# Every buffer that TensorE reads in the large products begins at a multiple of 2048 bytes

## The chip, the cores and the metric

The kernel runs on one core of one Trainium2 chip. The metric is device time in microseconds, the median of several runs. On the core, TensorE multiplies, VectorE and ScalarE work on the results and prepare operands, GpSimd does small work and issues some transfers, and SyncE issues the loads of the weights. All of them share an on-chip memory of 128 partitions; an address in this text is a byte offset inside a partition, the same in all 128.

## The reference

One inference step of a two-layer backbone over two streams of 128 tokens (context and latent) of width 1024. Each layer has a mixer (four kinds of attention behind one input projection of 2400 columns and one output projection) and a channel mixer: dense SwiGLU of width 2816 in layer 0, eight experts of width 3584 with two chosen per token in layer 1. Everything is float32.

```python
sh1, sc1, gt1, sh2, sc2, gt2 = _modulation(silu_cond, w_ada[l], b_ada[l])
h = _rmsnorm(x, norm_mix_pre[l]) * (1.0 + sc1) + sh1
x = x + gt1 * _rmsnorm(mixer(h) @ w_o[l], norm_mix_post[l])
h = _rmsnorm(x, norm_ffn_pre[l]) * (1.0 + sc2) + sh2
# layer 0: (silu(h @ wg) * (h @ wu)) @ wd ; layer 1: the same for 8 experts, summed with their gates
x = x + gt2 * _rmsnorm(channel_mixer(h), norm_ffn_post[l])
```

## The kernel before

**Units.** The weights come from HBM in units of [128, 2048] floats, 1 MB, into six raw buffers (`raw`, line 536 issues the loads on SyncE). A product of full precision is made of three fast ones: ScalarE rounds the unit to a high part (`w_hi`, line 841, `hi`), VectorE takes the difference as a low part (`w_lo`, line 1239, `lo`), and TensorE adds up high x high, low x high and high x low. The activations are split in the same way into `x_hi`, `x_lo` (1024 columns for each of two streams) and `h_hi`, `h_lo` (512 columns, the hidden layer).

**The products.** `products` (lines 1791 to 1800, experts and dense feed-forward) and `products_of` (lines 1802 to 1818, the projections and the last units of the dense stage) run over the tiles of a unit. Lines 1794/1809 multiply `x_hi` by `w_hi`, 1795/1810 `x_lo` by `w_hi`, and then, once the low part is there, 1799/1816 `x_hi` by `w_lo`. In each matmul the activation is the stationary operand, 128 x 128 (512 bytes per partition), and the weights are streamed through: 512 columns (2048 bytes) in the experts, the down units and the output projections, 256 in the dense gate and up units, 480 in the input projection. A unit of the experts is 4 tiles, so 8 high products and then 4 low ones.

**Slots.** A split unit lies in one of three slots; `slot(c)` (line 174) says which: slots 0 and 1 are in `w_hi` and `w_lo`, slot 2 is `w_hi3`, `w_lo3`, laid over `qz` (which attention uses), and slot 3, used once, lies in `region`. In the experts the slot is `-c % 3`. A block of the expert loop has the units up, up, down, down, gate, gate in TensorE's order after the transposes of line 2240, in slots 2, 1, 0, 2, 1, 0. In the dense stage gate units (before the transposes of line 2108) lie in slot 0, up units (after them) in slot 1, down units in slot 2, except the last down unit, which lies in slot 0.

**Where the buffers begin.** Buffers are laid one after the other, each rounded up to 32 bytes. The change puts 1920 bytes (`mod` 768, `small` 1024, `fill` 128) ahead of `raw` and asserts that the next address is a multiple of 2048, so memory begins 128 bytes past one. From the order of the declarations follow the distances past the last multiple of 2048:

| buffer | before | after |
|---|---|---|
| `raw`, `w_hi`, `w_lo` (slots 0, 1) | 128 | 0 |
| `region` (also slot 3 and `y_hi`, `y_lo`) | 128 | 0 |
| `w_hi3`, `w_lo3` over `qz` (slot 2) | 768 | 0 |
| `x_hi`, `x_lo` | 448 | 0 |
| `h_hi`, `h_lo` | 768 | 0 |
| `x`, `xn`, `cond`, `mrow` | 448 | 0 |
| `cst` (identity for the transposes) | 640 | 512 |

## Time and profile before

| | |
|---|---|
| median of 3 runs | 1540.9 us (1540.82 to 1544.19) |
| span of the profiled execution | 1541.9 us |
| TensorE matmuls | 1490.1 us busy, 97% |
| VectorE | 1155.6 us, 75% |
| ScalarE | 974.6 us, 63% |
| HBM | 317 GB/s over the span |

The stages in order of time are: the modulation and input projection of layer 0 (to about 75 us), attention and output projection (to 190), the dense feed-forward (190 to 376), layer 1 up to its router (376 to 558), the eight experts (558 to 1539). Matmuls are pipelined: a recorded matmul of 512 columns lasts about 390 ns, but the next one begins some 230 ns after it began. So the busy time of TensorE says that it is never idle, and not whether its matmuls follow each other as closely as they can. The chain that ended last is the view for that: it counts each piece from its beginning to the beginning of what follows.

### The profile page before, as it was taken

How to read it: one execution, taken by the hardware profiler on the slowest of the kernel's cores; microseconds unless marked ns; L12 is line 12 of the kernel's file. 1: busy time of each engine (PE TensorE's matmuls, PEld its weight loads, DVE VectorE, ACT ScalarE, POOL GpSimd, SP SyncE). 2: the span in 40 equal slices, each digit the busy share in tenths (PEclk: the TensorE clock that was granted, in tenths of full speed). 3: DMA queues.
4: the chain of work that ended last, by engine and by line, in shares of the span. 5: the costliest groups of instructions: out<-in, count | busy, mean ns of one | idle time of the engine just before them, and what ended most of it. 6: DMA issues, size and time to landing. Idle time of an engine off the chain costs nothing.

```text
span 1541.9 us, 21865 instructions
## 1 busy us (share of the span) xinstructions
PE 1490.1 (97%) x7705; PEld 1216.6 (79%) x7705; DVE 1155.6 (75%) x990; ACT 974.6 (63%) x959; POOL 125.2 (8%) x180
## 2 busy tenths in 40 slices
PE   6999999999998999999999999999999999999995
PEld 3867799996876788888878878878878887887884
DVE  2577554445667478888888888888888888888885
ACT  3555533445455457777777777777777777777773
POOL 2421410000021200000000000000000000000001
PEclk9999999999999899999999999999999999999998
DMA  8976986558661879999999999999999999999991
GB/s 327 343 267 200 333 264 198 174 189 290 241 211 60 323 279 366 396 365 392 367 346 394 375 355 382 374 356 373 381 369 360 385 369 357 386 371 342 395 386 50
DMA packets 222629, 489.13 MB, mean 317 GB/s; under 512 B 9040, under 2 KB 42144, under 8 KB 222576
## 3 DMA queue, kind: packets, MB, share of 16 engines
q1 hardware_dynamic: 215024, 466.38, 83.6%
q0 software_dynamic: 7552, 22.03, 4.7%
q8 instruction: 34, 0.56, 0.1%
q14 instruction: 19, 0.16, 0.0%
HBM read 479.53 MB, written 8.85 MB: 317 GB/s over the span
## 4 chain that ended last, share of the span: by engine, by line
PE 93%; DVE 3%; ACT 2%; issue 1%; DMA 1%; POOL 0%; POOLq 0%; SPq 0%; DVEq 0%; ACTq 0%
PE ps L1794 24%; PE ps L1799 24%; PE ps L1795 24%; PE ps L1809 4%; PE ps L1816 3%; PE ps L1810 3%; PE ps L1840 2%; PE ps L2240 2%; PE ps L2019 1%; DMA raw<-in_w_ada 1%; PE ps L1972 1%; PE ps L1851 1%; PE ps L1994 1%; PE ps L1896 1%; PE ps L1863 1%
## 5 line engine op out<-in xcount | busy, mean ns | idle before, releaser
L1239 DVE TENSOR_TENSOR w_lo<-raw,w_hi 128x2048 fp32r<-128x2048 f32 (+1 forms) x397 | 905.4, 2285 | 192.1 <-ACT w_hi L841 191.8
L841 ACT ACTIVATE w_hi<-raw 128x2048 fp32r<-128x2048 f32 (+1 forms) x397 | 757.8, 1914 | 255.7 <-PE ps L1795 236.2
L1794 PE MATMUL ps<-w_hi,x_hi 128*128 128x512 f32 (+1 forms) x1216 | 434.7, 369 | 1.4 <-DVE region L1465 1.4
L1795 PE MATMUL ps<-w_hi,x_lo 128*128 128x512 f32 (+1 forms) x1216 | 426.9, 363 | 0.0
L1799 PE MATMUL ps<-w_lo,x_hi 128*128 128x512 f32 (+1 forms) x1216 | 284.6, 364 | 0.0
L1794 PEld LDWEIGHTS ps<-w_hi,x_hi 128*128 128x128 f32 x1216 | 228.8, 188 | 40.6 <-DVE region L1465 1.6
L1795 PEld LDWEIGHTS ps<-w_hi,x_lo 128*128 128x128 f32 x1216 | 228.8, 188 | 36.4
L1799 PEld LDWEIGHTS ps<-w_lo,x_hi 128*128 128x128 f32 x1216 | 206.9, 188 | 39.6
L1794 PE MATMUL ps<-w_hi,h_hi 128*128 128x512 f32 x520 | 204.6, 393 | 4.9 <-DVE h_lo L1579 4.3
L1795 PE MATMUL ps<-w_hi,h_lo 128*128 128x512 f32 x520 | 204.3, 393 | 0.0
L1799 PE MATMUL ps<-w_lo,h_hi 128*128 128x512 f32 x520 | 139.0, 392 | 0.0
L1794 PEld LDWEIGHTS ps<-w_hi,h_hi 128*128 128x128 f32 x520 | 97.7, 188 | 28.2 <-issue 5.7
L1799 PEld LDWEIGHTS ps<-w_lo,h_hi 128*128 128x128 f32 x520 | 97.9, 188 | 21.5
L1795 PEld LDWEIGHTS ps<-w_hi,h_lo 128*128 128x128 f32 x520 | 97.8, 188 | 21.5
L1809 PE MATMUL ps<-w_hi,x_hi 128*128 128x480 f32 (+2 forms) x256 | 96.4, 382 | 5.0 <-ACT x_hi L906 4.5
L1810 PE MATMUL ps<-w_hi,x_lo 128*128 128x480 f32 (+2 forms) x256 | 94.6, 375 | 0.0
L1816 PE MATMUL ps<-w_lo,x_hi 128*128 128x480 f32 (+2 forms) x256 | 63.9, 374 | 0.0
L1809 PEld LDWEIGHTS ps<-w_hi,x_hi 128*128 128x128 f32 x256 | 49.1, 192 | 18.2 <-ACT x_hi L906 6.1
L809 POOL DMA_INDIRECT region<-h_rows,from_row x7 | 8.4, 1196 | 635.4 <-PE ps L2205 635.1
L1810 PEld LDWEIGHTS ps<-w_hi,x_lo 128*128 128x128 f32 x256 | 49.0, 191 | 7.0
L1840 PE MATMUL ps<-raw,cond 128*32 128x512 f32 x384 | 51.7, 639 | 2.8 <-DMA raw<-in_w_ada 1.9
L982 ACT ACTIVATE h_hi<-ps 128x512 fp32r<-128x512 f32 x11 | 6.6, 601 | 74.8 <-PE ps L2108 74.8
(271 smaller groups left out, 1086.6 us busy)
## 6 DMA issues: line engine op xcount, KB each, us to landing
raw<-in_moe_w_gate SPq DMA_DIRECT2D x112, 1024.0 KB, 7.3
raw<-in_moe_w_up SPq DMA_DIRECT2D x112, 1024.0 KB, 7.3
raw<-in_moe_w_down SPq DMA_DIRECT2D x112, 1024.0 KB, 7.2
raw<-in_w_ada SPq DMA_DIRECT2D x48, 1024.0 KB, 7.5
raw<-in_w_in SPq DMA_DIRECT2D x20, 960.0 KB, 7.7
raw<-in_ffn_w_gate SPq DMA_DIRECT2D x11, 1024.0 KB, 5.4
raw<-in_ffn_w_up SPq DMA_DIRECT2D x11, 1024.0 KB, 6.4
raw<-in_ffn_w_down SPq DMA_DIRECT2D x11, 1024.0 KB, 5.3
```

What stands on the lines that cost most here:

```text
L841: act.activation(split_hi(c, slice(0, width(c))), raw[:, r % NRAW, 0:width(c)], ACT.Copy).then_inc(hi_done, 1)
L1239: dve.tensor_sub(split_lo(c, n), raw[:, raw_of(c) % NRAW, n], split_hi(c, n)).then_inc(lo_done, 1)
L1794: pe.matmul(out, xh, split_hi(c, w), start=start, stop=False, skip_group_check=True)
L1795: last = pe.matmul(out, xl, split_hi(c, w), start=False, stop=False, skip_group_check=True)
L1799: last = pe.matmul(out, xh, split_lo(c, w), start=False, stop=stop, skip_group_check=True)
L1809: pe.matmul(out, xh, split_hi(c, w), start=start, stop=False, skip_group_check=True)
L1810: last = pe.matmul(out, xl, split_hi(c, w), start=False, stop=False, skip_group_check=True)
L1816: last = pe.matmul(out, xh, split_lo(c, w), start=False, stop=stop, skip_group_check=True)
L1840: last = pe.matmul(row_ps(m)[CG * kt:CG * kt + CG, :], cond[:, 4 * h + kt, i, :], raw[:, r % NRAW, 512 * kt:512 * kt + 512], start=first, ...
L1851: last = pe.matmul(col_ps(l, k)[:, 4 * kt:4 * kt + 4], mrow[:, m % 2, P * kt:P * kt + P], cst[:, C_SEL:C_SEL + 4], start=True, stop=True)
L1863: last = pe.transpose(ps[:, T_bank(l, which, s) + k // 4, cols(k % 4, P)], xn[:, s, cols(k, P)], ident())
L2240: last = pe.transpose(ps[:, 0, cols(r, P)], hid[:, cols(r, P)], ident())
```

## The change

The list of allocations is reordered and nothing else is edited: `mod`, `small` and an unused buffer `fill` of 128 bytes stand first, so that `raw` begins at a multiple of 2048; then come `raw`, `w_hi`, `w_lo`, `qz` (with `w_hi3`, `w_lo3`), `x_hi` (with `probs`), `x_lo`, `h_hi`, `h_lo`, `x`, `xn`, `cond`, `mrow`, whose sizes are all multiples of 2048, then `region`, and the small buffers behind it. Instructions, their order, shapes, waits and transfers stay as they are; only addresses differ.

```diff
+BLOCK_B = 2048
...
+        mod = sb("mod", [P, DEPTH, 6, KT, 2])
+        small = sb("small", [P, 256])
+        sb("fill", [P, 32])
+        assert nc.sbuf_base % BLOCK_B == 0, nc.sbuf_base
         raw = sb("raw", [P, NRAW, UNIT])
         w_hi = sb("w_hi", [P, NSPL - 1, UNIT], F32R)
         w_lo = sb("w_lo", [P, NSPL - 1, UNIT], F32R)
+        qz_at = nc.sbuf_base
+        qz = sb("qz", [P, 6, 2, 4, P])
+        w_hi3 = nc.alloc_sbuf_tensor_at("w_hi3", [P, UNIT], F32R, offset=qz_at)
+        w_lo3 = nc.alloc_sbuf_tensor_at("w_lo3", [P, UNIT], F32R, offset=qz_at + 4 * UNIT)
+        x_hi_at = nc.sbuf_base
+        x_hi = sb("x_hi", [P, 2, D], F32R)
+        probs_all = nc.alloc_sbuf_tensor_at("probs", [P, 2, 2, 4, 256], F32, offset=x_hi_at)
+        x_lo = sb("x_lo", [P, 2, D], F32R)
+        h_hi = sb("h_hi", [P, 512], F32R)
+        h_lo = sb("h_lo", [P, 512], F32R)
+        x = sb("x", [P, 2, D])
+        xn = sb("xn", [P, 2, D])
+        cond = sb("cond", [P, KT, 2, CG])
+        mrow = sb("mrow", [P, 2, 512])
+        assert nc.sbuf_base % BLOCK_B == 0, nc.sbuf_base
         REGION = 11904
         region_at = nc.sbuf_base
         region = sb("region", [P, REGION])
...
         cst = sb("cst", [P, C_N])
-        x = sb("x", [P, 2, D])
-        xn = sb("xn", [P, 2, D])
-        x_hi_at = nc.sbuf_base
-        x_hi = sb("x_hi", [P, 2, D], F32R)
...
-        x_lo = sb("x_lo", [P, 2, D], F32R)
-        cond = sb("cond", [P, KT, 2, CG])
-        mrow = sb("mrow", [P, 2, 512])
-        mod = sb("mod", [P, DEPTH, 6, KT, 2])
...
-        small = sb("small", [P, 256])
...
-        qz_at = nc.sbuf_base
-        qz = sb("qz", [P, 6, 2, 4, P])
...
-        h_hi = sb("h_hi", [P, 512], F32R)
-        h_lo = sb("h_lo", [P, 512], F32R)
```

## Rows read from the trace of the kernel before

**Rows 1.** The page: busy time, the chain by engine and line, loads

```profile
PE 1490.1 (97%) x7705; PEld 1216.6 (79%) x7705; DVE 1155.6 (75%) x990; ACT 974.6 (63%) x959; POOL 125.2 (8%) x180
...
PE 93%; DVE 3%; ACT 2%; issue 1%; DMA 1%; POOL 0%; POOLq 0%; SPq 0%; DVEq 0%; ACTq 0%
PE ps L1794 24%; PE ps L1799 24%; PE ps L1795 24%; PE ps L1809 4%; PE ps L1816 3%; PE ps L1810 3%; PE ps L1840 2%; PE ps L2240 2%; PE ps L2019 1%; DMA raw<-in_w_ada 1%; PE ps L1972 1%; PE ps L1851 1%; PE ps L1994 1%; PE ps L1896 1%; PE ps L1863 1%
...
raw<-in_moe_w_down SPq DMA_DIRECT2D x112, 1024.0 KB, 7.2
raw<-in_w_ada SPq DMA_DIRECT2D x48, 1024.0 KB, 7.5
```

**Rows 2.** Busy time by stage, with granted clock, DMA share and GB/s

```profile
core 0: us, PE busy (x) PEld busy (x) DVE busy (x) ACT busy (x) POOL busy (x), PEclk, DMA share, GB/s
...
190.00:376.00 186.00, 182.94 (x1325) 169.86 (x1327) 90.20 (x61) 72.19 (x58) 9.45 (x18) 1.00 0.66 217
...
520.00:541.00 21.00, 19.48 (x119) 15.19 (x117) 9.57 (x27) 13.81 (x24) 4.77 (x10) 0.71 0.88 325
541.00:558.00 17.00, 15.78 (x78) 13.83 (x78) 12.42 (x20) 10.06 (x8) 0.00 (x0) 0.86 0.60 211
558.00:1539.00 981.00, 962.55 (x4311) 783.08 (x4309) 844.30 (x486) 704.68 (x470) 30.50 (x23) 0.99 0.98 359
600.00:640.00 40.00, 40.00 (x181) 32.57 (x180) 34.70 (x19) 29.54 (x21) 0.00 (x0) 1.00 1.04 393
```

**Rows 3.** Waits, 700 to 1400 us, load queue apart: total, times, longest

```profile
ACT w_hi L841 <- PE ps L1795: 174.1, 230, 0.9
DVE w_lo L1239 <- ACT w_hi L841: 90.4, 197, 1.0
...
PE ps L1794 <- DVE h_lo L1579: 4.3, 6, 0.7
...
SPq L536 <- DVE w_lo L1239: 537.3, 241, 4.9
```

**Rows 4.** Chain in order of time, one expert block: start us, us

```profile
602.71 0.44 PE ps L2240 x4
...
604.99 0.92 PE ps L1799 x4
...
607.76 0.93 PE ps L1799 x4
...
610.55 0.94 PE ps L1799 x4
...
613.32 0.91 PE ps L1799 x4
...
616.09 0.93 PE ps L1799 x4
...
618.89 0.94 PE ps L1799 x4
619.83 0.44 PE ps L2240 x4
```

**Rows 5.** Chain, dense stage: up, down, gate, up, gate, the last down

```profile
204.30 1.81 PE ps L1799 x16
...
209.74 1.81 PE ps L1799 x8
...
215.32 1.89 PE ps L1799 x16
...
221.64 1.89 PE ps L1799 x16
...
232.76 1.89 PE ps L1799 x16
...
372.08 0.93 PE ps L1816 x4
```

**Rows 6.** Chain: input projection (480 columns), output projection (512 columns)

```profile
81.84 0.87 PE ps L1816 x4
...
163.44 0.93 PE ps L1816 x4
```

**Rows 7.** Chain: the first load

```profile
2.33 15.26 DMA raw<-in_w_ada
```

**Rows 8.** Timeline of ScalarE and VectorE in the experts: start us, us

```profile
737.66 1.92 ACT L841 ACTIVATE w_hi<-raw 128x2048 fp32r<-128x2048 f32 x1 [0.86 <-PE ps L1795]
...
736.93 2.29 DVE L1239 TENSOR_TENSOR w_lo<-raw,w_hi 128x2048 fp32r<-128x2048 f32 x1 [0.47 <-ACT w_hi L841]
...
744.63 0.68 DVE L1579 TENSOR_TENSOR h_lo<-ps,h_hi 128x512 fp32r<-128x512 f32 x1
```

More of the change, by code:

```diff
@@ L270, in program @@
         cst = sb("cst", [P, C_N])
-        x = sb("x", [P, 2, D])
-        xn = sb("xn", [P, 2, D])
-        x_hi_at = nc.sbuf_base
-        x_hi = sb("x_hi", [P, 2, D], F32R)
-        probs_all = nc.alloc_sbuf_tensor_at("probs", [P, 2, 2, 4, 256], F32, offset=x_hi_at)
-        x_lo = sb("x_lo", [P, 2, D], F32R)
-        cond = sb("cond", [P, KT, 2, CG])
-        mrow = sb("mrow", [P, 2, 512])
-        mod = sb("mod", [P, DEPTH, 6, KT, 2])
         mtmp = sb("mtmp", [P, KT, 2])
@@ L288, in program @@
         lam = sb("lam", [P, 8])
-        qz_at = nc.sbuf_base
-        qz = sb("qz", [P, 6, 2, 4, P])
-        w_hi3 = nc.alloc_sbuf_tensor_at("w_hi3", [P, UNIT], F32R, offset=qz_at)
-        w_lo3 = nc.alloc_sbuf_tensor_at("w_lo3", [P, UNIT], F32R, offset=qz_at + 4 * UNIT)
-        h_hi = sb("h_hi", [P, 512], F32R)
-        h_lo = sb("h_lo", [P, 512], F32R)
         pos = sb("pos", [P, 2, 2, NE + 1])
```

## The prediction

> **What bounds the kernel now.** I read the page first, then the busy time by stage, then the waits, then the chain in order of time. TensorE's matmuls are busy 1490.1 of 1541.9 us and the chain that ended last is 93% TensorE, three quarters of it the six lines that multiply by the split weights [rows 1]. By stage, the expert stage (558 to 1539) holds 981 us with matmuls busy for 962.55, the dense feed-forward stage 186 us with 182.94 [rows 2]. In the experts nobody makes TensorE wait: six waits for `h_lo`, 4.3 us in 700 us; ScalarE, VectorE and the load queue all wait for somebody who waits for TensorE [rows 3]. So the end is set by how far apart the starts of the matmuls lie, not by their recorded duration (393 ns), which overlaps the next one. I call that distance the pitch. The chain gives it, since it counts each matmul only until the next starts.
>
> **What the pitch depends on.** A block of the expert loop runs from transposes to transposes, 602.71 to 619.83: 17.12 us, of which 0.44 is the four transposes and 16.68 is 72 products, 231.7 ns each [rows 4]. The four low products at the end of each unit take 0.92, 0.93, 0.94, 0.91, 0.93, 0.94 us. That is an order of three. By the slot rule the six units (up, up, down, down, gate, gate) lie in slots 2, 1, 0, 2, 1, 0: the two short ones are the two in slot 2. Slots 0 and 1 begin 128 bytes past a multiple of 2048, slot 2 begins 768 past, which is a multiple of 256. The stationary columns begin at 448 plus multiples of 512 for `x_hi` (0.92) and at 768 plus multiples of 512 for `h_hi` (0.91). So both on multiples of 256 gives the shortest.
>
> The dense stage says it better. Its down units stand in slot 2 with `h_hi`: eight products in 1.81 us, 226.3 ns each. Only the last one stands in slot 0, with the same stationary buffer and lengths (it goes through `products_of`, four low products at a time): 0.93 for four, 232.5 [rows 5]. That pair is the ground of this forecast: move the streamed weights from 128 to a multiple of 256, in step with the stationary columns, and the pitch falls by about 6 ns. At 256 columns there are two speeds at the very same addresses: the up units at 204.30 and 221.64 take 1.81 and 1.89 us for sixteen, 113.1 or 118.1 ns [rows 5]. So an offset of 128 does not force the slow pitch; it lets the stream fall into it. Nothing in the trace begins at 0 with stationary columns at 0. The nearest row is the one at 768 with 768: equal offsets, as every product with 512 columns will have after the change.
>
> **The change, part by part.** It adds no instruction and no wait; all times come from the pitch.
> - *Experts.* 8 experts x 42 units x 12 = 4032 products. From 231.7 to 226.3 is 5.4 ns, 21.8 us in all. That is the upper end of what the rows support; the lower end is zero, and below zero in the rival. I take 85% of it, since a unit right after transposes or a wait needs a few products to fall into step: 18.5 us.
> - *Dense stage.* 11 gate and 11 up units x 48 = 1056 products of 256 columns, at 118.1 in the gate units (215.32, 232.76) and some up units, at 113.1 in the rest. If 14 of the 22 units lose 5.0 ns per product: 14 x 48 x 5.0 = 3.4 us at most; down units gain nothing. Taken: 2.2.
> - *Output projections.* Two layers x 4 units x 2 streams x 12 = 192 products at 232 [rows 6], 5.7 ns each: 1.1 us, taken 1.0; between layers the neighbours can take part of it.
> - *Input projections.* 480 products of 480 columns at 217.5 ns [rows 6]; scaled from 226.3 the good pitch is 212.2, so 2.5 us at most. But a chunk begins every 1920 bytes, so of four chunks the second and fourth will lie 128 past a multiple of 256, where before it was the first and third. Taken: 0.3, bounds -2.5 and 2.5.
> - *Loads.* `raw` moves from 128 to 0. The loads wait in the chain once, 15.26 us before the first matmul [rows 7]. The median loads of 1024 KB differ by 4% between their kinds, 7.2 and 7.5 us [rows 1], and 4 to 6% of 15.26 is under 1 us: taken 0, bounds -1 and 1. The Trainium skill ("DMA: Bandwidth & Descriptors", How a descriptor splits into AXI transactions) says that a descriptor which doesn't start on 256 bytes needs one transaction more: for rows of 2048 bytes 68 beats instead of 64, if it holds for the written side too. By that the first wait would be an estimated 0.9 us shorter. No row here compares the two.
> - *Everything else that is moved* (`cst`, `small`, `mod`, `xn`, the gaps in `region`): transposes run at 0.44 us for four, 110 ns, much longer than their 128 columns would need at this stream's rate, so the start of `cst` hardly shows. VectorE's and ScalarE's passes have the same shapes: 0. For a price if wrong: 56 blocks x 0.44 us = 25 us of transposes, 5% of it 1.2 us either way.
>
> Sum: 18.5 + 2.2 + 1.0 + 0.3 = 22.0 us. The profiled execution of before has a span of 1541.9, the median of the three runs is 1540.9, so a profile of after should have a span near 1519.9 and the median should be 1518.9.
>
> **Who is late next.** A block would last 17.12 - 72 x 0.0054 = 16.73 us. ScalarE needs 6 x 1.92, VectorE 6 x 2.29 = 13.7 plus two or three passes of 0.68, about 15.3 [rows 8]: both fit. Loads: 6.29 MB per block need 16.0 us at the 393 GB/s that the stage reaches when it has fallen behind, against 359 on the mean [rows 2]. They still fit, with 0.7 us to spare where there was 1.1. At expert boundaries the queue runs dry and the reserve is eaten; I leave 0 for it and up to 3 us as a bound. The clock: TensorE's granted clock is 0.71 and 0.86 in the stretches 520 to 541 and 541 to 558 [rows 2], a share of them at 1.2 GHz while the router runs. With all that comes before some 3 us earlier, the low stretch may shift against the products; bound 3 us either way.
>
> **Rivals.**
> - *No effect of the start.* Then the slots differ by something else that stays (the second operand's distance, the bank of the result, what the other engines write at the time) and the time stays 1540.9. The Trainium skill ("TensorE: Matmul & The Clock Gate", Part 2) has TensorE read the streamed and the stationary operand through two independent ports, so that loading the next columns takes nothing from the running matmul; and "SBUF — State Buffer" (Operand start alignment) asks only for a multiple of the element size, and says that this is about legality, not speed. By these pages the result is this rival. What speaks against it is the last down unit of the dense stage against the ten before it [rows 5]; what speaks for it is that identical addresses show both 113 and 118 ns [rows 5].
> - *Slower: everything in step is the bad case.* The mechanism is a clash between the streamed columns and the stationary columns read at the same time. If it depends on the absolute start and not on equal offsets, then buffers that all begin at 0 clash in all three slots, and slot 2 loses what it has. Price: 112 slot 2 units in the experts x 12 x (234 - 228.7) = 7.1 us; 10 down units x 24 x 6.2 = 1.5; eight quick up units x 48 x 5.0 = 1.9. Together 10.5, so 1551.4. It decides as soon as the low products of slot 2 take 0.93 or more. For it: in slots 0 and 1 the second chunk of 480 columns begins exactly at a multiple of 2048 (128 + 1920), and that stage runs at 217.5 ns where 212.2 would be the good rate. Against it: 768 with 768 is just as much in step, and it is the best case of the trace.
> - *Half of it.* Only the streamed operand counts: all units behave like slot 2 does now, 0.92 with `x_hi` in four of six and 0.91 with `h_hi` in two, 229.2 on the mean. 4032 x 2.5 = 10.1, plus half of the rest, 12 us: 1529.
> - *More than the trace has ever shown.* If 226.3 is itself held up by the streamed buffer crossing a multiple of 2048 (768 + 2048 crosses one, 0 + 2048 doesn't), the pitch could go towards 512 / 2.4 = 213 ns. Then loads would set a block at 16.0 us: 56 x 1.1 = 62 us at most, and about half of it with the boundaries: 1505 or so.
>
> **How the numbers follow.** The forecast has a chance of 0.55; half of it 0.12; no effect 0.12; slower 0.14; more 0.07. A difference of 0.3% (4.6 us) is about what a measurement of this kernel tells from none. Faster by more than that: 0.55 + 0.12 + 0.07 = 0.74; within it 0.12; slower 0.14. The forecast's own range is 1513 to 1527 (85% taken as 60% to 100%, the 3 us of the clock and the 3 us of the loads). To hold 8 in 10 the range reaches down to 1511 and up past no effect to 1542; what is left out is the slower case and most of the much faster one, 0.19.
>
> **What would show it.** In the chain of after, the low products of the six units of a block should read 0.91 each instead of 0.92, 0.93, 0.94, and transposes to transposes 16.7. The dense stage's sixteen should read 1.81 in up as in gate, and its last down unit 0.91 for four. Wrong would be: blocks of 17.12 (no effect); low products of 0.93 or 0.94 in slot 2 (slower); waits of ScalarE for `raw` in the experts (loads are the bound); a low clock in a stretch where it was full.

## The result, and the profile after

The changed kernel takes 1527.2 us (median of 4 runs, 1526.15 to 1529.33) where the kernel before took 1542.6 beside it (4 runs): a ratio of 0.990 [0.9886, 0.9911], 15.4 us less. The forecast was 1518.9, 22.0 us below the 1540.9 known then. The profiled executions have spans of 1524.5 and 1541.9, 17.4 apart.

The page of after, busy time and the chain by engine. It answers [rows 1]; every line number is 4 higher, so L1798 is what L1794 was.

```profile
PE 1471.9 (97%) x7705; PEld 1216.1 (80%) x7705; DVE 1153.6 (76%) x990; ACT 974.4 (64%) x959; POOL 124.9 (8%) x180
...
PE 92%; DVE 3%; ACT 2%; issue 1%; DMA 1%; POOL 0%; POOLq 0%; SPq 0%; DVEq 0%; ACTq 0%
```

The same instructions in the same numbers, and TensorE still sets the end. VectorE and ScalarE are as busy as before; only TensorE's 7705 matmuls are shorter, by 18.2 us.

The chain in order of time, one expert block (start us, us, what), answering [rows 4]:

```profile
601.56 0.44 PE ps L2244 x4
...
603.85 0.91 PE ps L1803 x4
...
606.57 0.91 PE ps L1803 x4
...
609.29 0.91 PE ps L1803 x4
...
612.01 0.91 PE ps L1803 x4
...
614.73 0.91 PE ps L1803 x4
...
617.45 0.91 PE ps L1803 x4
618.36 0.44 PE ps L2244 x4
```

All six units of the block now show 0.91 for their four low products, and transposes to transposes is 16.80 us instead of 17.12. The next block has a 0.92 in its first unit, which comes right after the transposes. Over the blocks of the trace the five later units run at 226.7 ns a product. The first unit, which starts slowly behind the transposes, has 237.2 on the mean where it had 236.8: it gained nothing.

The chain in the dense stage, an up unit, a down unit, a gate and an up unit, then the last down unit, answering [rows 5]:

```profile
201.94 1.92 PE ps L1803 x16
...
207.51 1.81 PE ps L1803 x8
...
213.16 1.92 PE ps L1803 x16
...
219.57 1.92 PE ps L1803 x16
...
373.35 0.92 PE ps L1820 x4
```

Here the forecast fails: sixteen products of 256 columns take 1.92 us, 120 ns each, where before some units showed 1.81 and others 1.89. The down units keep their 1.81 for eight, and the last one fell from 0.93 to 0.92.

Busy time by stage, as [rows 2] (us, busy time and count of each engine, granted clock, DMA share, GB/s): the dense stage, the experts, and 40 us of the experts:

```profile
190.00:376.00 186.00, 183.62 (x1299) 171.19 (x1300) 88.31 (x59) 71.36 (x56) 5.91 (x12) 1.00 0.62 206
...
558.00:1522.00 964.00, 944.96 (x4310) 781.60 (x4308) 842.38 (x486) 704.56 (x470) 30.05 (x23) 0.99 0.98 366
590.00:630.00 40.00, 40.00 (x181) 33.10 (x181) 35.72 (x20) 29.79 (x19) 0.00 (x0) 1.00 1.04 414
```

In the same 186 us TensorE began 1299 matmuls where it had begun 1325. The last line says that the loads, when they have fallen behind and run without a break, move 414 GB/s; before it was 393 in [rows 2] and is 394 in this stretch (its line stands at the end of the experiments).

**Where the 17.4 us went.** Times from the starts of the first and last matmul of each kind, in both traces, in us:

| stretch | before | after | difference | forecast |
|---|---|---|---|---|
| start to first product of 480 columns | 27.69 | 25.60 | -2.1 | 0 |
| input projection, layer 0 | 59.84 | 58.99 | -0.85 | -0.3 (both layers) |
| attention, output projection, layer 0 | 91.96 | 91.83 | -0.1 | -0.5 |
| dense stage, 256-column products first to last | 182.68 | 187.03 | **+4.35** | **-2.2** |
| last dense product to the end of layer 1's input projection | 75.77 | 75.51 | -0.3 | 0 |
| attention, output projection, router, layer 1 | 109.83 | 108.58 | -1.25 | -0.5 |
| experts, first to last product | 976.67 | 959.32 | **-17.35** | **-18.5** |
| end | 17.46 | 17.63 | +0.2 | 0 |

The mean pitch (start of a matmul to the start of the next, within runs of the same length) gives the same: products with `x_hi`, `x_lo` in the experts 232.0 to 227.4 ns, with `h_hi`, `h_lo` 230.7 to 226.9, output projections 232.3 to 227.9, dense products of 256 columns 115.6 to 119.8. 2688 x 4.6 + 1344 x 3.8 ns are 17.5 us in the experts, and 1056 x 4.2 ns are 4.4 us in the dense stage.

### The profile page after: what moved, and what is told of

Same layout as the page of the kernel before. It is cut to its first block, busy times and chain, and to the rows that moved or that the text cites. A ratio compares the mean times of both kernels' runs of the same rounds, so it can differ in the third digit from the quotient of the medians.

```text
span 1524.5 us, 21865 instructions
## 1 busy us (share of the span) xinstructions
PE 1471.9 (97%) x7705; PEld 1216.1 (80%) x7705; DVE 1153.6 (76%) x990; ACT 974.4 (64%) x959; POOL 124.9 (8%) x180
## 4 chain that ended last, share of the span: by engine, by line
PE 92%; DVE 3%; ACT 2%; issue 1%; DMA 1%; POOL 0%; POOLq 0%; SPq 0%; DVEq 0%; ACTq 0%
PE ps L1798 24%; PE ps L1799 24%; PE ps L1803 24%; PE ps L1813 4%; PE ps L1814 3%; PE ps L1820 3%; PE ps L1844 2%; PE ps L2244 2%; PE ps L2023 1%; DMA raw<-in_w_ada 1%; PE ps L1976 1%; PE ps L1998 1%; PE ps L1900 1%; PE ps L1855 1%; PE ps L1867 1%
## 5 line engine op out<-in xcount | busy, mean ns | idle before, releaser
L1798 PE MATMUL ps<-w_hi,x_hi 128*128 128x512 f32 (+1 forms) x1216 | 432.1, 366 | 1.4 <-DVE region L1469 1.4
L1798 PEld LDWEIGHTS ps<-w_hi,x_hi 128*128 128x128 f32 x1216 | 229.6, 189 | 36.5 <-DVE region L1469 1.6
L1798 PE MATMUL ps<-w_hi,h_hi 128*128 128x512 f32 x520 | 203.3, 391 | 4.9 <-DVE h_lo L1583 4.3
L1798 PEld LDWEIGHTS ps<-w_hi,h_hi 128*128 128x128 f32 x520 | 97.7, 188 | 26.2 <-issue 5.7
```

The costliest lines, as they stand in the source:

```text
L1798: pe.matmul(out, xh, split_hi(c, w), start=start, stop=False, skip_group_check=True)
```

## What the experiments had to tell

Three readings were left. The absolute start counts: a multiple of 256 or of 2048 bytes is what helps. Or only the difference between the starts of the stationary and of the streamed operand counts. Or neither: what the other engines read and write at the time shifts with the addresses. From here on "distance" is the start of the stationary columns minus the start of the streamed ones, modulo 256 bytes. Times stand beside runs of the kernel before on the same chip. A kernel's edit is against after unless it says otherwise.

### All at 128, and one of the two moved

All in step, but 128 bytes past a multiple of 256 (`e1_all128`; the two asserts go as well):

```diff
-        sb("fill", [P, 32])
+        sb("fill", [P, 64])
```

> The changed kernel with all its buffers moved 128 bytes further on (128 more bytes ahead of raw), so that streamed and stationary operands still begin at equal offsets, but at 128 past a multiple of 2048 instead of 0. Theory A (equal offsets count, the absolute start doesn't): the low products of an expert block read 0.91 us in all six units, the sixteen low products of the dense gate and up units 1.92, the span is that of the changed kernel, 1524.5 within 2 us. Theory B (the absolute multiple counts, as the change says): 0.93 to 0.94 as in slots 0 and 1 before, span 1540 or more.

Only the streamed weights at 128, all three slots, everything else at 0 (`e2_w128`):

```diff
         raw = sb("raw", [P, NRAW, UNIT])
+        sb("pad1", [P, 32])
         w_hi = sb("w_hi", [P, NSPL - 1, UNIT], F32R)
         w_lo = sb("w_lo", [P, NSPL - 1, UNIT], F32R)
         qz_at = nc.sbuf_base
         qz = sb("qz", [P, 6, 2, 4, P])
...
+        sb("pad2", [P, 480])
         x_hi_at = nc.sbuf_base
```

> The changed kernel with only the streamed weights (w_hi, w_lo and slot 2) moved to 128 past a multiple of 2048; x_hi, x_lo, h_hi, h_lo and everything behind stay at 0. Theory A (equal offsets): the pitch rises, low products 0.93 or more in all six units of an expert block, dense gate and up units below 1.92 because the distance is no longer 0; span 1535 to 1545. Theory B (absolute multiple of the streamed operand) says the same for the experts. If only the start of the stationary operand counted, everything would stay at 0.91 and 1524.5.

Only the stationary `x_hi`, `x_lo`, `h_hi`, `h_lo` at 448 (`e3_x448`):

```diff
+        sb("pad1", [P, 112])
         x_hi_at = nc.sbuf_base
...
         h_lo = sb("h_lo", [P, 512], F32R)
+        sb("pad2", [P, 400])
         x = sb("x", [P, 2, D])
```

> The changed kernel with only the stationary operands (x_hi, x_lo, h_hi, h_lo) moved to 448 past a multiple of 2048, where x_hi began before; the streamed weights stay at 0. Theory A (equal offsets): low products of the experts 0.92 to 0.94, dense gate and up units 1.81 to 1.89 instead of 1.92, span 1527 to 1540. If only the streamed operand's multiple counts: 0.91 in all six units of an expert block, span within 3 us of 1524.5, dense unchanged at 1.92.

| | time, us | ratio | experts, us | dense, us |
|---|---|---|---|---|
| all at 128 | 1530.4 | 0.9919 [0.989, 0.9948] | 959.39 | 187.0 |
| streamed at 128 | 1548.5 | 1.0035 [1.002, 1.0051] | 979.72 | 187.06 |
| stationary at 448 | 1531.0 | 0.9918 [0.9894, 0.9942] | 966.49 | 182.26 |

Three chains in order of time, each with low products of an expert unit and sixteen of the dense stage. All at 128:

```profile
214.49 1.92 PE ps L1801 x16
...
604.49 0.91 PE ps L1801 x4
```

Streamed at 128:

```profile
214.31 1.90 PE ps L1805 x16
...
600.58 0.94 PE ps L1805 x4
```

Stationary at 448:

```profile
213.99 1.82 PE ps L1805 x16
...
604.77 0.92 PE ps L1805 x4
```

With everything at 128 the experts and the dense stage are those of after to 0.1 us: between 0 and 128 the absolute start doesn't count. The span, 1528.2, is 3.7 us above the 1524.5 that was expected within 2; where they lie is said under the clock. Streamed at 128 the span is 1546.6, a little above the expected range. With one operand moved against the other the stages follow, and not both in the same order: distance 0 is the best of the three in the experts but no better than distance 128 (streamed at 128) in the dense stage, and distance 192 (stationary at 448) is in the middle in the experts and the best in the dense stage. The dense stage holds both lengths: its products of 256 columns run at 118.8 ns at distance 128 against 119.8 in after, and its down units, of 512 columns, take back what that gains. At distance 192 the mean is 114.9 ns, and 14 of the stage's 24 stretches of these products, gate and up alike, end at 113.3.

### The distance by itself

To take the other engines out, a kernel that only runs chains of matmuls in the order of `products`, from two buffers filled with a constant, on TensorE alone; outputs are zeros and nothing of the reference is computed. The other engines are done before the first pair of starts begins. Its loop, with `m` and `s` the starts of the streamed and the stationary columns (`p1_grid`):

```python
for k in range(n):
    wk = w[:, m + W * k:m + W * k + W]
    pe.matmul(o, xs[:, 0, s + P * k:s + P * k + P], wk, ...)
    pe.matmul(o, xs[:, 1, s2 + P * k:s2 + P * k + P], wk, ...)
for k in range(n):
    pe.matmul(o, xs[:, 0, s + P * k:s + P * k + P], w[:, 4096 + m + W * k:4096 + m + W * k + W], ...)
```

> Not the model: nothing of the reference is computed, the outputs are filled with zeros. TensorE alone repeats the kernel's pattern of products (high x high, low x high, then high x low; stationary 128 columns, streamed 512 or 256) three times for each pair of starts, streamed at 0, 64, 128, 256, 384, 768, 1024 (512 columns) or 0 to 512 (256 columns), stationary at 0 to 448 in steps of 64, four transposes between the pairs. No other engine writes meanwhile. Theory A (equal offsets): the pitch at 512 columns is the same along lines of equal distance and lowest, 226.7 ns, at distance 0; at 256 columns 120 ns at distance 0 and 113 to 118 elsewhere. Theory B (absolute multiples of 256): 226.7 only where the streamed start is a multiple of 256. Theory C (what the other engines write at the time makes the difference): 226.7 everywhere.

The chain of this kernel in order of time: low products with both starts at 0, then, after four transposes, with the stationary columns 64 bytes further:

```profile
45.20 0.91 PE ps L81 x4
46.11 0.44 PE ps L72 x4
...
48.42 0.93 PE ps L81 x4
...
54.02 0.93 PE ps L81 x4
```

Pitch in ns from the starts, 56 pairs of starts at 512 columns (streamed at 0, 64, 128, 256, 384, 768, 1024) and 48 at 256 columns, in the last of the three rounds that each pair runs (the first, right after the transposes, is slower at every distance):

| distance | 0 | 64 | 128 | 192 |
|---|---|---|---|---|
| 512 columns | 226.6 | 233.1 | 231.8 (up to 233.7 in four pairs) | 228.9 |
| 256 columns | 120.0 | 117.8 (113.3 in three of twelve pairs) | 118.8 (120.0 in one) | 117.8 |

At distances 0 and 192 rows agree to 0.3 ns whatever the start of the streamed columns is, beyond 256 bytes too; at 128, and at 64 with 256 columns, a few pairs stand apart. No other engine works while these chains run, so the others are not the cause of the differences between them.

The distance explains most of the kernel before without a free number. Slots 0 and 1 with `x_hi` lie 448 - 128 = 320 apart, distance 64: 233. Slot 2 with `x_hi`: 448 - 768, distance 192: 229. Two up and two gate units stand in slots 2, 1, 1, 0, so the mean should be (229 + 3 x 233) / 4 = 232.0; measured 232.0. Slot 2 with `h_hi`, distance 0: 226.6, the dense stage's 226.3 of [rows 5]. It does not explain the down units of the experts: slot 0 with `h_hi` is distance 128 and slot 2 distance 0, which makes 229.2 on the mean, and 230.7 was measured. The unit in slot 0 has 232.5 as it should; the one in slot 2, which follows it without a pause, has 229.0 and not 226.6, while in after, where all neighbours have distance 0 too, it has 226.7. What runs just before counts as well.

### Finer, and the order of what comes before

The same kernel with steps of 16 bytes, 480 columns, different starts for the high and the low stationary columns, and 256 columns once after transposes and once straight behind 512-column products (`p2_fine`):

```diff
+COMBOS = [(0, s, s, 256, 3, 1) for s in range(0, 256, 16)] + \
+    [c for s in range(0, 256, 16) for c in ((0, 0, 0, 512, 2, 1), (0, s, s, 256, 3, 0))] + \
+    [(0, s, s, 512, 3, 1) for s in range(0, 256, 16)] + \
+    [(0, s, s, 480, 3, 1) for s in range(0, 256, 32)] + \
+    [(0, s, s2, 256, 3, 1) for s in range(0, 256, 64) for s2 in range(0, 256, 64)]
```

> Again only TensorE's pattern of products, outputs are zeros. Streamed at 0, stationary from 0 to 240 in steps of 16, at 256 columns (once right after transposes, once right after 24 products of 512 columns without a pause), at 512 and 480 columns, and at 256 columns with the two stationary operands (high and low part) at different starts, 0, 64, 128 or 192 each. Theory A: at 512 columns a curve of the distance with its minimum of 226.7 only at 0 and a jump to 231 or more within one or two steps; at 256 columns 120 at distance 0 and at least one distance where 113.3 is reached however the sequence begins. Theory D (256 columns have two states at any distance but 0 and the start decides): the two series at 256 columns differ at the same distance.

| distance | 0 | 16 | 48 | 64 | 80 | 128 | 176 | 192 | 208 | 240 |
|---|---|---|---|---|---|---|---|---|---|---|
| 512 columns | 226.6 | 233.4 | 233.4 | 233.5 | 232.3 | 233.0 | 229.5 | 228.6 | 233.3 | 226.7 |
| 256 columns after transposes | 120.0 | 118.3 | 117.8 | **113.3** | 118.7 | 118.9 | 118.1 | 117.8 | 116.7 | 117.2 |

At 512 columns 0 and 240 are alone at the bottom, and 176 to 192 is a second, higher one. At 480 columns every distance gives 216 to 220. At 256 columns there are two speeds for the same addresses. The chain in order of time, distance 64 after transposes:

```profile
72.92 0.44 PE ps L75 x4
...
75.19 0.91 PE ps L84 x8
...
77.91 0.91 PE ps L84 x8
...
80.63 0.91 PE ps L84 x8
```

and the same distance straight behind products of 512 columns:

```profile
243.10 0.91 PE ps L84 x4
...
245.89 0.94 PE ps L84 x8
...
248.72 0.94 PE ps L84 x8
...
251.55 0.94 PE ps L84 x8
```

Eight in 0.91 are 113.3 ns each, eight in 0.94 are 117.8. Neither speed gives way to the other within 72 products. That is the 1.81 beside 1.89 at the same addresses in [rows 5]. But transposes or no transposes is not what decides: both up units of [rows 5] follow transposes, and the first of these two kernels (`p1_grid`) has the very same pair, streamed at 0 and stationary at 64, at 117.8 ns right after four transposes:

```profile
536.26 0.44 PE ps L72 x4
...
538.58 0.94 PE ps L81 x8
```

Nor is distance 64 alone in this: distance 192 has 117.8 in every row of the grid, but 113.3 in most units of the kernel with the stationary columns at 448, gate units straight behind products of 512 columns among them. What decides between the two stays open. With the high columns at distance 64 and the low ones at 192, 113.3 comes from the first products on, with 192 and 64 from the second round on, the first having 118.7; the other pairs of different starts have 116.8 to 119.1.

### What of the change is needed

Two pads in the kernel before, 384 bytes, and its order of memory otherwise (`e4_old_order`). All operands of the experts, the down units and the output projections then lie at distance 0, none at a multiple of 256:

```diff
         xn = sb("xn", [P, 2, D])
+        sb("pad1", [P, 48])
         x_hi_at = nc.sbuf_base
...
         lam = sb("lam", [P, 8])
+        sb("pad2", [P, 48])
         qz_at = nc.sbuf_base
```

> The kernel before with its old order of the memory and nothing at a multiple of 2048: 192 unused bytes ahead of x_hi and 192 ahead of qz, so that x_hi, x_lo begin at 640, slot 2, h_hi and h_lo at 1152, and slots 0 and 1 stay at 128. All the distances between streamed and stationary starts are then multiples of 256. Theory A as the grid puts it (only the distance modulo 256 bytes counts): the gain of the change comes back in full with 384 bytes of padding: low products of the experts 0.91 in all units, dense gate and up units 1.92 for sixteen, span within 4 us of 1524.5, ratio to the kernel before 0.989 to 0.992. If the order, the multiples of 2048 or 512 counted: low products of 0.92 to 0.94 in part of the units and a time above 1532.

Measured 1530.3 us, ratio 0.9905 [0.9883, 0.9926]; experts 959.40 us, dense stage 187.04, pitches 226.9 and 227.4 as in after. The span, 1529.3, is 0.8 us above what was expected, for the same reasons as with all at 128. The new order and the multiple of 2048 are not needed for what the experts gain. What after has beyond this is in the loads and the clock, below.

After once more, unedited, as the base of the next three (`e0_after`):

> The changed kernel again, unedited, as the yardstick on the same chip for the two that follow. Both theories: the same as on record, 1526 to 1530 us, dense stage 187.0 us from its first to its last product of 256 columns, experts 959.3.

1528.4 us, 0.9907 [0.9891, 0.9924].

### The dense stage given back

If distance 64 at 256 columns can reach 113.3 ns, the gate and up units have to lie 192 bytes further, and nothing else (`e5_dense64`; the slots are made 64 floats longer):

```diff
+        def at(c, n):
+            o = 48 if FFN_U + 2 <= c < MOE_U and SPLIT[c][2] < 3 * NFF - 1 and (SPLIT[c][2] + 1) % 3 < 2 else 0
+            return slice(n.start + o, n.stop + o)
...
-            return w_hi[:, slot(c), n] if slot(c) < 2 else w_hi3[:, n]
+            return w_hi[:, slot(c), at(c, n)] if slot(c) < 2 else w_hi3[:, n]
```

> The changed kernel, but gate and up units of the dense stage in slots 0 and 1 are written and read 192 bytes into their slot (slots are 256 bytes longer), so that the stationary operands begin 64 past the streamed ones modulo 256, as before the change, in this stage only; all products of 512 columns keep distance 0. Theory A (distance modulo 256, and 256 columns want another distance than 512): the dense stage goes back to 182.7 us from 187.0 (pitch 115.7 instead of 119.9, some units at 113, some at 118), experts stay at 959.3, the whole is 4.3 us quicker than the changed kernel. If the loss in the dense stage came from something else in the new order, it stays at 187.0.

Then `x_lo` of the dense stage 128 bytes further, for the pair of 64 and 192 (`e6_dense_best`):

```diff
+        def lo_at(l, which, n):
+            o = 32 if which and not l else 0
+            return slice(n.start + o, n.stop + o)
...
-            def xcols(s, k):
-                return x_hi[:, s, P * k:P * k + P], x_lo[:, s, P * k:P * k + P]
+            def xcols(s, k, dense=False):
+                o = 32 if dense else 0
+                return x_hi[:, s, P * k:P * k + P], x_lo[:, s, P * k + o:P * k + P + o]
```

> As the kernel before this one, and besides x_lo is written and read 128 bytes further on in the dense stage, so that the high stationary part begins 64 and the low one 192 past the streamed start, the pair that gave 113.3 ns from its first products on in the second grid. Theory A: the pitch at 256 columns is 113.4 in all but the first two units, the sixteen low products 1.81 us in up and gate units alike, dense stage 180.3 us, the whole 6.5 us quicker than the changed kernel. Theory D (two states at the same distance, the start decides): gate units, which follow products of 512 columns without a pause, stay at 117.8 and only up units reach 113.3; then 182 to 183 us.

In both of these the condition also caught layer 1's projection units in slots 0 and 1, which was not meant: layer 1's output projections ran at 232.3 ns instead of 227.6 to 228.0. The third has the condition mended and the two slots apart, gate units 192 bytes in (distances 64 and 192), up units 64 bytes in (192 and 64) (`e7_dense_two`):

```diff
+            o = 0
+            if FFN_U + 2 <= c < MOE_U and SPLIT[c][0] == "ffn" and SPLIT[c][2] < 3 * NFF - 1:
+                o = (48, 16, 0)[(SPLIT[c][2] + 1) % 3]
```

> As the last kernel (x_lo 128 bytes further on in the dense stage), but with a start of its own for each kind of unit: gate units 192 bytes into their slot, so that the stationary parts begin 64 and 192 past the streamed start, up units 64 bytes into it, so that they begin 192 and 64 behind it modulo 256. Projection units of layer 1, which the last two kernels had moved 192 bytes as well, are back at distance 0. Theory D (which pair of distances reaches 113.3 ns depends on how the unit begins; the grid has 192 and 64 at 113.3 right after transposes): up units reach 113.3 within their first ten products, gate units as before, dense stage 180.5 us or less, output projection of layer 1 back at 227 ns, whole 1521 to 1523 us, 6 us quicker than the changed kernel. Theory A alone says nothing about the order of the two; if the start isn't what decides, up units stay at 120 in their high products and the dense stage at 183.

| | time, us | ratio | dense, us | mean pitch, ns |
|---|---|---|---|---|
| after, edited nowhere | 1528.4 | 0.9907 [0.9891, 0.9924] | 187.03 | 119.8 |
| 64 for both | 1524.2 | 0.9877 [0.986, 0.9893] | 182.59 | 115.7 |
| 64 and 192 | 1524.0 | 0.9879 [0.9862, 0.9895] | 182.99 | 116.1 |
| two slots apart | 1523.7 | 0.9861 [0.9844, 0.9878] | 181.37 | 114.4 |

The chain of each in order of time, one gate and one up unit. Distance 64 for both:

```profile
212.18 1.89 PE ps L1807 x16
...
218.36 1.81 PE ps L1807 x16
```

64 and 192:

```profile
211.27 1.81 PE ps L1811 x16
...
217.58 1.83 PE ps L1811 x16
```

Two slots apart:

```profile
214.17 1.82 PE ps L1813 x16
...
220.28 1.81 PE ps L1813 x16
```

The first gives up units 113.3 and gate units 117.8, as expected. The second missed the 180.3 of one reading; the other had named 182 to 183, but with slow gate and quick up units, and it came the other way round: gate units have 113.7 and 113.3 in high and low products, up units 120 in their high ones. In the third the low products are at 113.3 in all but the first four stretches, which the edit leaves where they were, and one more; it ends at 181.37 and 1523.7, not quite at the 180.5 and the 1521 to 1523 expected. So 4.0 to 5.7 us come back in the dense stage, the experts stay at 959.4 in all three, and the third is faster than both given kernels: its interval ends at 0.9878 where that of after, repeated, begins at 0.9891.

### Looking for the mechanism

If the loading of the stationary columns clashes with the stream, fewer stationary columns should clash less, and the curve over the distance should keep its place. If the streamed start has a part of its own, equal starts should differ. 128, 96, 64 and 32 stationary columns, equal starts at other steps, and the streamed start alone (`p3_cols`, again without the reference's computation):

```diff
+COMBOS = [(0, s, s, 512, 3, 1, C) for C in (128, 96, 64, 32) for s in (0, 64, 128, 192)] + \
+    [(m, m, m, 512, 3, 1, 128) for m in (16, 32, 48, 80, 112)] + [(m, 0, 0, 512, 3, 1, 128) for m in (16, 32, 48, 240)] + \
+    [(m, m, m, 256, 3, 1, 128) for m in (16, 32, 48)] + [(0, s, s, 256, 3, 1, 64) for s in (0, 64, 128, 192)]
```

> TensorE's pattern alone, outputs are zeros. 512 streamed columns with 128, 96, 64 or 32 stationary columns at distances 0, 64, 128, 192; equal starts that are not multiples of 64 (16, 32, 48, 80, 112) and streamed starts of 16, 32, 48, 240 with stationary at 0; 256 columns at equal starts of 16, 32, 48, and with 64 stationary columns. Theory E (what costs is the reading of the stationary columns beside the streamed ones, a clash that the distance decides): the excess over the lowest pitch shrinks with the stationary columns, from 6 ns at 128 to about 1.5 at 32, and 256 columns at distance 0 fall from 120 towards 115 with 64. Theory F (the distance acts on the streamed read alone): the excess doesn't depend on the number of stationary columns. Equal starts off 64: 226.7 if only the distance counts, more if a multiple of 64 is needed as well.

| stationary columns, 512 streamed | distance 0 | 64 | 128 | 192 |
|---|---|---|---|---|
| 128 | 226.6 | 233.1 | 231.8 | 228.9 |
| 96 | 230.2 | 228.6 | 226.6 | 233.1 |
| 64 | 229.6 | 233.0 | 230.8 | 228.5 |
| 32 | 231.7 | 231.7 | 230.1 | 231.9 |

The spread over the four distances is 6.5, 6.5, 4.5 and 1.8 ns. It shrinks at 64 and 32, as a clash with the stationary columns would have it, but not at 96, where the same 226.6 to 233.1 stand at other distances; and the level doesn't come down: 128 columns at distance 0 are quicker than 64 or 32 at any of the four. At 256 streamed columns 64 stationary ones have 113.3, 119.0, 116.8 and 116.6 at the four distances, so there distance 0, the worst with 128, is the best. Equal starts at 16, 32, 48, 80 and 112 bytes give 233.4, 226.6, 231.1, 229.8 and 230.2: distance 0 holds only where both starts are multiples of 32 (16, 48, 80 and 112 are not). The streamed start at 16, 32, 48 and 240 with the stationary one at 0 gives 231.8, 233.3, 233.5 and 236.9. Two of these are distances 240 and 16, which gave 226.7 and 233.4 with the streamed columns at 0: below steps of 32 bytes the distance alone doesn't settle the pitch. So neither a clash that only grows with the number of stationary columns nor the streamed start alone is the mechanism. What it is stays open. A pattern in which both reads must fit each other in time, so that length and start count together, would fit; it was not tested.

### The loads alone

Only `raw` moves to a multiple of 256, in the kernel before (`e8_raw0`); the 1920 bytes ahead of it shift everything behind by the same amount and leave every distance as it was:

```diff
+        sb("pad0", [P, 480])
         raw = sb("raw", [P, NRAW, UNIT])
```

> The kernel before in its old order with 1920 unused bytes ahead of raw, so that raw begins at a multiple of 2048 (and of 256) and everything behind it moves by the same 1920 bytes: no distance between streamed and stationary operands changes. Theory G (a load written to rows that begin off a multiple of 256 bytes is slower, as 413 GB/s with raw at 0 against 392 to 395 with raw at 128 in the kernels run so far suggests): 590 to 630 us reads 412 to 415 GB/s, the first load of the chain 14.1 to 14.5 us instead of 15.26, experts unchanged at 976.7 us since they don't wait for loads, the whole 1 to 3 us quicker than the kernel before, by a start that comes earlier. If the rate came from the products or the order of the buffers: 394 GB/s and 1542.

1540.9 us (11 runs, against 15 of the kernel before), ratio 0.9988 [0.9979, 0.9997], about 1.9 us less. The same 40 us of the expert stage, as in the last line of [rows 2] (the last number is GB/s). Before:

```profile
590.00:630.00 40.00, 40.00 (x178) 32.55 (x177) 35.10 (x20) 28.83 (x18) 0.00 (x0) 1.00 1.05 394
```

`raw` alone moved:

```profile
590.00:630.00 40.00, 40.00 (x178) 32.54 (x177) 34.99 (x19) 29.02 (x19) 0.00 (x0) 1.00 1.04 413
```

The old order with two pads, where `raw` stays at 128 and the products are quick:

```profile
590.00:630.00 40.00, 40.00 (x182) 33.07 (x181) 35.42 (x21) 30.26 (x21) 0.00 (x0) 1.00 1.04 392
```

The rate follows the start of `raw` and nothing else that was changed: 392 to 395 GB/s in the three traces with `raw` at 128 (before, all at 128, old order), 413 or 414 in the eight with it at a multiple of 256. The first load in the chain takes 15.26, 15.01 and 15.48 us there, 14.11 to 14.43 here. In the experts it is worth nothing (976.69 against 976.67), since they never wait for a load. The same number says once more that the starts themselves don't count there: all of them moved by 1920 bytes.

## Why the forecast was right, and where it was not

**Experts: right, 17.35 for 18.5.** The step from the last down unit in slot 0 against the ten in slot 2 [rows 5] was the right comparison, and 4032 products the right count. They lost 4.3 ns on the mean where 85% of 5.4 is 4.6. The remainder is where the text put it, in the products after transposes: the first unit of a block gained nothing, the other five run at 226.7. What the step called the cause, both on multiples of 256, was only a special case: both at the same distance from one is as good (all at 128). The change gives both at once, so the forecast didn't hang on which it is. But the time alone would not have told the forecast from its rival: 1527.2 lies just past the end of the forecast's own range, 1513 to 1527, and nearer to "half of it", 1529, than to 1518.9. The six times 0.91 in the block decide for the forecast's experts; the dense stage made the sum look like the rival's.

**Dense stage: wrong in sign, +4.35 for -2.2.** The step that failed is that equal offsets, best at 512 columns, were taken to be best at 256 as well: "equal offsets, as every product with 512 columns will have after the change" was carried over to a shape for which the trace had no such pair. All dense gate and up units of before stood at distance 64 [rows 5], which has a state at 113.3; at distance 0, with starts at multiples of 32, the runs with 128 stationary columns show only about 120. The prediction had read the two speeds at the same addresses correctly as two states and then assumed that the slow one would go. It was the good one that went. What could have warned: only one of the two lengths had an example with equal offsets, so the bounds of this term had to reach to a loss. The prediction priced one, 1.9 us, in a rival (the eight quick up units going to 118.1); the 120 stood nowhere in that trace.

**Input projections: -1.0 for -0.3**, within its bounds of 2.5. The pitch gives 0.4 of it, 217.15 to 216.25 ns over 480 products; the rest lies in the pauses between them. At 480 columns the distance changes with each chunk of 1920 bytes, and between the distances there are no more than 4 ns. The good pitch of 212.2 that was scaled from 512 columns is reached at none of the eight; the least round has 214.8. **Output projections:** 232.3 to 227.9, 192 x 4.4 ns = 0.8 us for 1.0.

**Loads: taken as 0, worth about 0.8 on the first one**, 15.26 to 14.42 us, with bounds of 1. From the Trainium skill ("DMA: Bandwidth & Descriptors", How a descriptor splits into AXI transactions), which speaks of what a transaction reads, the prediction had estimated 68 beats against 64 for the written side, a ratio of 1.06. The measured rates have 413 / 394 = 1.05, and the estimate of 0.9 us for the first wait stands beside 0.84. The sizes agree; that the splitting is the cause is not shown. With `raw` alone moved the first product of 480 columns comes 1.27 us earlier, of the 2.1. Neither number is clear of the variation: among the eight kernels with `raw` at a multiple of 256 that product begins between 24.4 and 26.8 us, and among the three others between 26.7 and 27.7.

**The clock, bound 3 us: used in part.** The granted clock of two stretches around layer 1's attention and router (columns as in [rows 2]). Before:

```profile
460.00:480.00 20.00, 16.12 (x124) 13.65 (x124) 18.13 (x55) 11.27 (x47) 1.89 (x4) 1.00 0.00 1
520.00:558.00 38.00, 35.26 (x195) 29.02 (x194) 22.00 (x47) 23.87 (x32) 4.77 (x10) 0.78 0.76 274
```

After:

```profile
460.00:480.00 20.00, 18.43 (x129) 16.50 (x128) 18.00 (x53) 10.01 (x43) 1.27 (x2) 0.83 0.00 1
520.00:558.00 38.00, 32.19 (x201) 26.01 (x200) 21.82 (x47) 24.50 (x35) 5.16 (x11) 0.87 0.76 275
```

All at 128:

```profile
520.00:558.00 38.00, 35.25 (x189) 29.42 (x188) 19.63 (x47) 21.51 (x31) 5.16 (x11) 0.73 0.68 240
```

In before TensorE's granted clock was at 0.5, the lower of its levels (1.2 GHz), for 17.1 us in the second stretch; in after for 10.2 us there and for 6.8 us in the first, where it had been full. That is the last of the signs of being wrong that the prediction named; it did come, though the stretch as a whole got no longer for it. From the end of layer 1's input projection to the first expert product it took 109.83 us before and 108.58 in after, with 17 us of low clock in both, and 111.08 with all at 128, where the clock was low for 6.8 us in the first and 20.5 us in the second stretch. That 2.5 us, and the 1.1 us by which its first product of 480 columns comes later, make up the 3.7 us between the profiled spans of all at 128 and after. The shift doesn't come from the layout of the operands as such: all at 128 and after have the same distances and differ in it.

**Who would be late next.** Nobody. TensorE's wait for `h_lo` is 4.3 us in six times, to the digit that of [rows 3]; ScalarE waits 162.6 us for TensorE where it waited 174.1. The loads kept their reserve: the blocks got only 0.3 us shorter, and the loads 5% quicker. The 3 us kept for them were not needed.

**The rivals.** No effect of the start, 0.12, fell with the experts. The Trainium skill ("TensorE: Matmul & The Clock Gate", Part 2) has two independent read ports and says that loading the stationary operand takes no read bandwidth from the running matmul; the runs show that its address matters all the same, 226.6 against 233.1 ns with no other engine at work. Everything in step is the bad case, 0.14, was half right: in step is the slowest at 256 columns (120.0, shared with distances 144 and 160) and the quickest at 512, but the price that it named, slot 2 losing what it had, didn't come, and the absolute start has no part in it at the starts of this kernel. Half of it, 0.12, fell, though its time was the nearer one: it had only the streamed operand count, with 0.92 in four of six units, and all six read 0.91; and moving the stationary operands alone made the experts 7.2 us longer (stationary at 448). More than the trace has ever shown, 0.07: 226.6 is the least that any pair of starts gave at 512 columns with TensorE alone.

In sum, the sign was right and so was the experts' term, its cause being equal offsets and not multiples of 256; of the 6.6 us between forecast and result in the median, or 4.6 in the spans, the dense term is 6.55 against it, and what the start, the clock and the input projection gave beyond their terms goes the other way.

## What to carry to other kernels

For matmuls of this kind (4-byte operands) that follow each other without a gap, the start of the stationary columns minus the start of the streamed ones, modulo 256 bytes, is a parameter of the layout, worth 3% at 512 columns and 6% at 256. Keep both starts at multiples of 32 bytes, the only ones for which equal starts gave 226.6 ns. The best value differs from one pair of lengths to another, so each stage of a kernel gets its own, and a good value is to be carried over to another shape only once it is measured there, in the kernel itself: which of two states a stage falls into was not foreseeable from the chains alone. Read it from the starts of the matmuls or the chain in order of time, never from the recorded durations. Buffers that loads write did best at multiples of 256 bytes.

## What the runs showed of the hardware that was not expected

- Pitch of back-to-back 4-byte matmuls with 128 stationary columns and nothing but the starts of the two operands (and what ran before) different: 226.6 to 236.9 ns at 512 streamed columns, 113.3 to 120.1 at 256, 216 to 220 at 480. 226.6 ns are 0.443 ns a column, 113.3 the same, 216 are 0.450.
- At 256 columns two states at the same addresses, 113.3 and 117.8 ns, each kept for 72 products: at distance 64 in the chains and in the kernel before, at distance 192 in the kernel with the stationary columns at 448, where the chains show only the second. Both occur right after transposes; what decides is open.
- The best of the four distances at 512 columns is 0 with 128 stationary columns, 128 with 96 and 192 with 64; at 256 columns with 64 stationary ones it is 0 (113.3); equal starts that aren't multiples of 32 bytes lose it (231.1 to 233.4 at 48 and 16).
- Loads of 1 MB in rows of 8192 bytes per partition to a start 128 bytes past a multiple of 256 run at 394 GB/s, at a multiple at 413.
